# First expert's weights loaded early in a fused S5 / mLSTM / MoE block on Trainium2

## The chip, the cores and the metric

One core of a Trainium2 (trn2) chip runs the whole program in one launch. The metric is the device time in microseconds, lower is better. The engines go by their short names: PE multiplies matrices, ACT and DVE work elementwise, POOL (GpSimd) does small work and the indexed transfers, SP (SyncE) only issues transfers. Each has its own instruction stream, they meet through semaphores, and an engine that waits holds back all that stands behind the wait in its stream.

## What is computed

The reference is one decoder block of width 1024 on 1024 tokens, in float32. What matters here is its last part, the mixture of experts:

```python
logits = t @ w_router + b_router            # t: (1024, 1024), 32 experts
top_vals, top_idx = lax.top_k(logits, 4)
gate = softmax(top_vals)
# for every expert e, over the tokens that chose it:
h = xb @ w_up[e] + b_up[e]                  # (tokens, 2048)
g = minimum(h[:, :1024], 7); lin = clip(h[:, 1024:], -7, 7)
act = g * sigmoid(1.702 * g) * (lin + 1)
y = act @ w_down[e] + b_down[e]             # (tokens, 1024), added to its tokens times gate
```

Ahead of it stand a norm, an input projection, two sequence mixers (mLSTM and S5), the output projection and the router; behind it a last norm.

## The kernel before

`hybrid_block` (L2928) runs five stages one after the other: `project`, `mlstm`, `s5`, `project_out_route` and `experts`. Each is a block of its own with a barrier of all engines at its end, and has its own tiles and semaphores; what must outlive a stage is in `keep_tiles` (L93) or, up to the router, in `mixer_tiles` (L111).

**The route stage**, `project_out_route` (L1523), multiplies the mixers' output by `w_out`, whose 16 pieces come through a ring of four (`raw`, L1531); the last low part of one is made by DVE at L1909 (semaphore `w_lo_done`). Then for each of eight token tiles it norms (result in the first half of `mix["sig_o"]`, called `normed`, stored to DRAM as `t` by SP at L1667), transposes (second half of `sig_o`, called `tT`), makes the logits (PE, L1816 and L1817, semaphore `logits_ready`), takes the top four, and POOL scatters token numbers into a table in DRAM (L1718). SP then stores the residual `h3` tile by tile (L1670), after the fourth of them loads the finished table into SBUF (L1673), and waits for that at the end.

**The expert stage**, `experts` (L2069), goes over the experts in order, in passes of one or two blocks of up to 128 tokens. A pass takes an expert's 12 MB of weights in `CHUNKS` = 12 chunks of 1 MB, 0 to 7 from `w_up` and 8 to 11 from `w_down`. Each chunk takes three steps: SP loads it into a ring of `RAW` = 6 tiles (`load`, L2281), ACT copies its high part into `w_hi` (`hi`, L2493, and `hi_ahead`, L2500; rings of `SPLIT` = 4), DVE makes the low part `w_lo` (`lo`, L2633), and PE multiplies with both (`multiply`, L2825, matmuls at L2868, L2869 and L2872, the bias row at L2878). A load waits for the low part of the chunk six before. The first expert's first six loads wait for nothing:

```python
def load(n, e, j):
    sp.wait_ge(lo_done, n * CHUNKS + (j + 1))
    sp.dma_start(raw[:, j % RAW, :, :], piece(e, j)).then_inc(raw_full[j % RAW], 16)
```

The stage starts with a prologue. POOL gathers the first expert's token rows (L2350) and then loads `b_up` twice into `bias_rows`, 32 rows in partitions 0 to 31 and again in 32 to 63 (L2449). PE turns the token rows (`first_x_turn`, L2897). ACT casts chunk 0 (L2498), makes the high part of the token rows (L2602), casts chunk 1, waits for the bias rows plus one, and copies them (L2607). DVE first waits for the bias rows (L2752) and adds one to a half (L2753), then makes chunk 0's low part (L2635), the token rows' low part (L2759), chunk 1's low part, and the bias rows' low part (L2764). PE's first matmul (L2868) waits for chunk 0's low part and for the token rows' low part. Inside the pass DVE's list, written out by hand in `item` (L2726), has chunk 10's low part at j = 6 ahead of the clamp and product of the hidden half (`hide`, L2685, ops at L2693 and L2700) at j = 7; PE turns that half at L2816 behind chunk 8.

`passes` (L2222) reads the plan of an expert into registers and branches to the pass bodies that it needs, on every engine.

## Time and profile before

| | |
|---|---|
| median of 3 runs | 2300.9 us (2299.7 to 2306.86) |
| the profiled execution's own time | 2290.0 us |
| its span, first to last instruction | 2287.9 us |
| mean granted PE clock | 0.974 of 2.4 GHz |
| PE busy | 2153.6 us, 94% of the span |
| DVE busy | 1616.2 us, 71% |
| ACT busy | 1212.0 us, 53% |
| POOL busy | 549.0 us, 24% |
| DMA | 541.61 MB, 237 GB/s mean |
| expert stage | from 599.2 us to the end |

Times inside the profile are microseconds from the span's start, "mean ns" apart. A row of the timeline has the start, the time (of a merged group), the engine, the line, the operation, output and inputs, and in brackets how long the engine was idle before and what ended it. "SPq" is SP's issuing. The profiled execution took 10.9 us less than the median of the runs, so what is summed from its rows is a difference, to be taken off either.

### The profile page before, as it was taken

Reading aid. Unit: us, or ns where it says so; the run is one execution under the profiler, and the core shown is the slowest. Engines: PE = TensorE matmul, PEld = TensorE weight load, DVE = VectorE, ACT = ScalarE, POOL = GpSimd, SP = SyncE. Lnnn points to the kernel's source line nnn. Section 1 sums busy time; section 2 is a strip of 40 time slices with the busy share of each in tenths; the row PEclk is TensorE's granted clock in tenths of the full one; section 3 lists DMA queues with packets and bytes.
Section 4 is the critical chain, followed back from the end, with each engine's and each line's share of the span. In section 5 each row is a group of like instructions: output and inputs, shape, how many; then the busy total and the mean of one; then the engine's idle time right before and its main releaser. Section 6 shows DMA issues by size and latency. Waiting matters only on the chain.

```text
span 2287.9 us, 32495 instructions
## 1 busy us (share of the span) xinstructions
PE 2153.6 (94%) x10442; PEld 1785.9 (78%) x10443; DVE 1616.2 (71%) x1858; ACT 1212.0 (53%) x1246; POOL 549.0 (24%) x521
## 2 busy tenths in 40 slices
PE   6999986799499999999999999999999999999996
PEld 6787975488378888888888888888888888888874
DVE  4688857546675665779579775877875687677766
ACT  4422243332354554667467564766755576565655
POOL 1001021204411110413134140512511243121304
PEclk9999988999599999999999999999999999999998
DMA  6123263431696675969689895988996699778877
GB/s 181 56 83 135 84 135 129 137 134 65 239 346 190 219 238 200 317 221 379 236 292 373 276 310 202 325 304 280 364 319 215 221 367 336 222 251 293 299 234 263
DMA packets 287300, 541.61 MB, mean 237 GB/s; under 512 B 37302, under 2 KB 53798, under 8 KB 286146
## 3 DMA queue, kind: packets, MB, share of 16 engines
q1 hardware_dynamic: 262770, 494.54, 62.2%
q0 software_dynamic: 24464, 46.24, 8.0%
q8 instruction: 35, 0.57, 0.1%
q14 instruction: 31, 0.25, 0.0%
HBM read 513.61 MB, written 65.13 MB: 253 GB/s over the span
## 4 chain that ended last, share of the span: by engine, by line
PE 56%; issue 6%; DVE 5%; DMA 3%; ACT 3%; ACTq 0%; DVEq 0%; SPq 0%; POOL 0%; POOLq 0%
PE ex_ps_l L2869 8%; PE ex_ps_l L2868 8%; PE ex_ps_g L2869 7%; PE ex_ps_g L2868 7%; PE ex_ps_y L2868 5%; PE ex_ps_y L2869 5%; PE ex_ps_l L2872 4%; PE ex_ps_g L2872 4%; PE ex_ps_y L2872 3%; DVE ex_w_lo L2635 3%; PE ex_ps_t L2806 2%; ACT ex_w_hi L2503 2%; PE ex_ps_t L2816 2%; PE ex_ps_l L2823 1%; DMA ex_raw<-in_w_down_dram 1%
## 5 line engine op out<-in xcount | busy, mean ns | idle before, releaser
L2635 DVE TENSOR_TENSOR ex_w_lo<-ex_raw,ex_w_hi 128x2048 fp32r<-128x2048 f32 x408 | 926.7, 2289 | 371.1 <-ACT ex_w_hi L2503 303.6
L2503 ACT CAST ex_w_hi<-ex_raw 128x2048 fp32r<-128x2048 f32 x371 | 706.4, 1910 | 275.6 <-PE ex_ps_g L2869 99.5
L2342 POOL TENSOR_TENSOR ex_passed<-keep_ident 128x1 f32<-128x1 f32 x136 | 133.6, 982 | 1171.9 <-ACT ex_y L2546 1133.4
L2868 PE MATMUL ex_ps_g<-ex_w_hi,ex_x_hi 128*128 128x512 f32 x784 | 307.3, 392 | 13.0 <-DVE ex_x_lo L2759 11.1
L2868 PE MATMUL ex_ps_l<-ex_w_hi,ex_x_hi 128*128 128x512 f32 x784 | 308.6, 394 | 2.6 <-DVE ex_w_lo L2635 2.6
L2869 PE MATMUL ex_ps_g<-ex_w_lo,ex_x_hi 128*128 128x512 f32 x784 | 305.7, 390 | 0.0
L2869 PE MATMUL ex_ps_l<-ex_w_lo,ex_x_hi 128*128 128x512 f32 x784 | 305.5, 390 | 0.0
L2868 PE MATMUL ex_ps_y<-ex_w_hi,ex_h_hi 128*128 128x512 f32 x544 | 217.5, 400 | 1.7 <-DVE ex_h_lo L2671 1.0
L2869 PE MATMUL ex_ps_y<-ex_w_lo,ex_h_hi 128*128 128x512 f32 x544 | 212.3, 390 | 0.0
L2872 PE MATMUL ex_ps_g<-ex_w_hi,ex_x_lo 128*128 128x512 f32 x544 | 212.2, 390 | 0.0
L2872 PE MATMUL ex_ps_l<-ex_w_hi,ex_x_lo 128*128 128x512 f32 x544 | 212.1, 390 | 0.0
L2868 PEld LDWEIGHTS ex_ps_g<-ex_w_hi,ex_x_hi 128*128 128x128 f32 x784 | 147.6, 188 | 44.0 <-DVE ex_x_lo L2759 11.5
L2868 PEld LDWEIGHTS ex_ps_l<-ex_w_hi,ex_x_hi 128*128 128x128 f32 x784 | 147.2, 188 | 34.6 <-DVE ex_w_lo L2635 5.1
L2869 PEld LDWEIGHTS ex_ps_g<-ex_w_lo,ex_x_hi 128*128 128x128 f32 x784 | 147.6, 188 | 30.1
L2869 PEld LDWEIGHTS ex_ps_l<-ex_w_lo,ex_x_hi 128*128 128x128 f32 x784 | 147.3, 188 | 29.5
L2872 PE MATMUL ex_ps_y<-ex_w_hi,ex_h_lo 128*128 128x512 f32 x424 | 166.0, 391 | 0.0
L2868 PEld LDWEIGHTS ex_ps_y<-ex_w_hi,ex_h_hi 128*128 128x128 f32 x544 | 102.2, 188 | 24.5 <-DVE ex_h_lo L2671 4.9
L2872 PEld LDWEIGHTS ex_ps_g<-ex_w_hi,ex_x_lo 128*128 128x128 f32 x544 | 102.5, 188 | 21.4
L2872 PEld LDWEIGHTS ex_ps_l<-ex_w_hi,ex_x_lo 128*128 128x128 f32 x544 | 102.1, 188 | 21.4
L2869 PEld LDWEIGHTS ex_ps_y<-ex_w_lo,ex_h_hi 128*128 128x128 f32 x544 | 102.3, 188 | 19.7
L2350 POOL DMA_INDIRECT keep_x_rows<-t,ex_gather_at x68 | 110.7, 1628 | 22.3 <-issue 20.6
L601 PE MATMUL pr_acc<-pr_h_hi,pr_w_hi 128*128 128x512 f32 (+1 forms) x240 | 94.8, 395 | 3.9 <-DVE pr_h_lo L655 1.6
(483 smaller groups left out, 3699.0 us busy)
## 6 DMA issues: line engine op xcount, KB each, us to landing
ex_raw<-in_w_up_dram SPq DMA_DIRECT2D x272, 1024.0 KB, 9.2
ex_raw<-in_w_down_dram SPq DMA_DIRECT2D x136, 1024.0 KB, 8.3
st_tab<-tabs SPq DMA_DIRECT2D x8, 1408.0 KB, 7.4
pr_raw<-in_w_in_dram SPq DMA_DIRECT2D x10, 1024.0 KB, 5.5
tabs<-keep_x_rows POOLq DMA_DIRECT2D x16, 256.0 KB, 2.3
tabs<-keep_x_rows SPq DMA_DIRECT2D x16, 256.0 KB, 2.0
por_raw<-in_w_out_dram SPq DMA_DIRECT2D x16, 256.0 KB, 5.3
t<-mix_sig_o SPq DMA_DIRECT2D x8, 512.0 KB, 2.6
```

What stands on the lines that cost most here:

```text
L601: pe.matmul(to, w_hi[:, s, k, cols], h_hi[:, k, toks], start=(k == 0), stop=False)
L2342: pool.tensor_tensor(passed[:, :], ident[:, 0:1], ident[:, 0:1], ALU.add).then_inc(passed_done, 1)
L2350: pool.indirect_dma_start(out=x_rows[:, b, :], out_offset=None, in_=t_dram, in_offset=bass.IndirectOffsetOnAxis(ap=gather_at[:, b:b + 1], ...
L2503: nc.scalar.copy(w_hi[:, j % SPLIT, :, :], raw[:, j % RAW, :, :]).then_inc(hi_done, 1)
L2635: v.tensor_tensor(w_lo[:, j % SPLIT, :, :], raw[:, j % RAW, :, :], w_hi[:, j % SPLIT, :, :].bitcast(F32), ALU.subtract).then_inc(lo_done, 1)
L2806: mm = pe.transpose(to[:, k * P:(k + 1) * P], x_rows[:, b, (4 * half + k) * P:(4 * half + k + 1) * P], ident[:, :])
L2816: mm = pe.transpose(to[:, k * P:(k + 1) * P], hidden[:, row(half, b, blocks), k * P:(k + 1) * P], ident[:, :])
L2823: pe.matmul(to[:, :], lo_in[:, b, 4 * part + k, :], w_hi[:, s, k, :], start=False, stop=False)
L2868: pe.matmul(to[:, :], hi_in[:, b, kk, :], w_hi[:, s, k, :], start=first, stop=False)
L2869: mm = pe.matmul(to[:, :], hi_in[:, b, kk, :], w_lo[:, s, k, :], start=False, stop=last and b > 0)
L2872: mm = pe.matmul(to[:, :], lo_in[:, b, kk, :], w_hi[:, s, k, :], start=False, stop=last)
```

## The change

`EARLY` = 3 chunks of the first expert get their tiles in `keep`, and are loaded in the route stage. `sig_o` moves from `mixer_tiles` to `keep_tiles`, and a new tile `weights` of 1 MB is added there. The other stages, which had tiles of that size of their own, use it too (the second slot of `project`'s weight ring stays its own, the first one is `weights`; `normed` of `mlstm`; `w` of `s5`; the `w_out` ring of the route stage). SP in the route stage loads chunk 0 into `weights` once the last low part of `w_out` is made, chunk 1 into the second half of `sig_o` once all logits are made, and chunk 2 into its first half once the stores of `t` have landed; both of these stand behind the first store of `h3`. In the expert stage SP loads the bias rows ahead of its loop, and for pass number 0 leaves out chunks 0 to 2, by a branch on the pass number that every pass of the loop evaluates. ACT and DVE have the prologue in another order.

```diff
+EARLY = 3
...
 def keep_tiles(nc, ctx):
...
+        "sig_o": sb("sig_o", [P, HEADS, T], F32),
+        "weights": sb("weights", [P, 4, 512], F32),
+        "raw_full": [sem(f"raw_full{i}") for i in range(EARLY)],
...
+def early_tile(keep, j):
+    if j == 0:
+        return keep["weights"][:, :, :]
+    return keep["sig_o"][:, 4 - 2 * j:6 - 2 * j, :].rearrange("p a (b n) -> p (a b) n", n=512)
...
 # project_out_route
-        raw = sb("raw", [P, RING, HALF], F32)
+        raw = keep["weights"]
...
+                sp.wait_ge(w_lo_done, 2 * KD)
+                sp.dma_start(early_tile(keep, 0), weights(p, 0, 0)).then_inc(keep["raw_full"][0], 16)
                 for j in range(TT):
                     sp.wait_ge(scaled, j + 1)
                     sp.dma_start(t_t[:, j, :], normed[:, j % 2, :]).then_inc(normed_out[j % 2], 16)
                 for j in range(TT):
                     sp.wait_ge(acc_read, TT + 2 * j + 2)
                     sp.dma_start(h3_t[:, j, :], h2(j)).then_inc(h3_out, 16)
+                    if j == 0:
+                        sp.wait_ge(logits_ready, TT)
+                        sp.dma_start(early_tile(keep, 1), weights(p, 0, 1)).then_inc(keep["raw_full"][1], 16)
+                        for b in range(2):
+                            sp.wait_ge(normed_out[b], 16 * TT // 2)
+                        sp.dma_start(early_tile(keep, 2), weights(p, 0, 2)).then_inc(keep["raw_full"][2], 16)
                     if j == PLACES_AT:
...
-                for b in range(2):
-                    sp.wait_ge(normed_out[b], 16 * TT // 2)
                 sp.wait_ge(places_in, 16)
...
 # experts: weights(p, e, j) is the old piece(e, j), raw(j) the tile of chunk j
-        raw = sb("raw", [P, RAW, 4, 512], F32)
+        late = sb("late", [P, RAW - EARLY, 4, 512], F32)
...
                 def one_pass(n, e, blocks, plan, kind=None, small=False):
-                    for j in range(CHUNKS):
+                    if e is LAST_E:
+                        for j in range(EARLY):
+                            load(n, e, j)
+                    else:
+                        n = sp.snap(n)
+                        with sp.If(n > 0):
+                            for j in range(EARLY):
+                                load(n, e, j)
+                    for j in range(EARLY, CHUNKS):
                         load(n, e, j)
...
+                for i in range(2):
+                    sp.dma_start(bias_rows[i * E:(i + 1) * E, :], p["b_up"][0]).then_inc(bias_in, 16)
                 with sp.Fori(0, E - 1) as e:
...
                 gather(0, 0, 1)
-                for i in range(2):
-                    pool.dma_start(bias_rows[i * E:(i + 1) * E, :], p["b_up"][0]).then_inc(bias_in, 16)
...
                 hi(0, 0, False)
+                hi(0, 1, False)
+                act.wait_ge(h3_out, 16 * TT)
+                act.wait_ge(bias_plus, 1)
+                nc.scalar.copy(bias_hl[0:2 * E, :], bias_rows[0:2 * E, :]).then_inc(bias_hi_set, 1)
                 for half in range(2):
                     act.wait_ge(t_full, half + 1)
                     nc.scalar.copy(x_hi[:, 0, 4 * half:4 * half + 4, :],
                                    ps_t[half][:, :].rearrange("p (k t) -> p k t", k=4)).then_inc(t_hi, 1)
-                hi(0, 1, False)
-                act.wait_ge(h3_out, 16 * TT)
-                act.wait_ge(bias_plus, 1)
-                nc.scalar.copy(bias_hl[0:2 * E, :], bias_rows[0:2 * E, :]).then_inc(bias_hi_set, 1)
                 hi(0, 2, False)
...
                 choose(0, 0)
+                lo(0, 0)
                 v.wait_ge(bias_in, 32)
                 v.tensor_scalar(bias_rows[0:2 * E, F:2 * F], bias_rows[0:2 * E, F:2 * F], 1.0, None, ALU.add).then_inc(bias_plus, 1)
-                v.wait_ge(bias_plus, 1)
-                lo(0, 0)
+                lo(0, 1)
                 for half in range(2):
...
-                lo(0, 1)
                 v.wait_ge(h3_out, 16 * TT)
+                v.wait_ge(bias_plus, 1)
                 v.wait_ge(bias_hi_set, 1)
```

## Rows read from the trace of the kernel before

**Rows 1.** The chain that ended last, in the expert stage's start (start us, us, what).
```profile
599.40 0.69 SPq L2224
...
600.59 0.47 issue
...
629.76 13.12 DMA ex_raw<-in_w_down_dram
```

**Rows 2.** Busy time by stretch: us, then each engine's, granted PE clock, DMA share, GB/s.
```profile
620.00:640.00 20.00, 20.00 (x88) 16.43 (x87) 18.47 (x11) 13.69 (x10) 0.00 (x0) 0.96 1.04 386
```

**Rows 3.** Timeline of the expert stage's prologue.
```profile
600.65 0.17 ACT L2598 COPY ex_warm<-keep_row_pick 128x1 f32<-128x1 f32 x1
...
602.89 1.10 POOL L2449 DMA_DIRECT2D ex_bias_rows<-in_b_up_dram  x2
...
605.08 1.96 PE L2901 MATMUL ex_ps_t<-keep_ident,keep_x_rows 128*128 128x128 f32 x8 [8.34 <-DMA keep_x_rows<-t,ex_gather_at]
...
607.78 1.90 ACT L2498 CAST ex_w_hi<-ex_raw 128x2048 fp32r<-128x2048 f32 x1 [6.95 <-DMA ex_raw<-in_w_up_dram]
...
609.59 1.06 ACT L2602 CAST ex_x_hi<-ex_ps_t 128x512 fp32r<-128x512 f32 x2
...
613.83 0.73 DVE L2753 TENSOR_SCALAR ex_bias_rows<-ex_bias_rows 64x1024 f32<-64x1024 f32 x1 [14.29 <-DMA ex_bias_rows<-in_b_up_dram]
...
616.41 1.89 ACT L2607 CAST ex_bias_hl<-ex_bias_rows 64x2048 fp32r<-64x2048 f32 x1
616.81 1.28 DVE L2759 TENSOR_TENSOR ex_x_lo<-ex_ps_t,ex_x_hi 128x512 fp32r<-128x512 f32 x2
...
618.14 0.79 PE L2868 MATMUL ex_ps_g<-ex_w_hi,ex_x_hi 128*128 128x512 f32 x1 [11.10 <-DVE ex_x_lo L2759]
```

**Rows 4.** Timeline, end of the first pass.
```profile
642.97 1.90 ACT L2503 CAST ex_w_hi<-ex_raw 128x2048 fp32r<-128x2048 f32 x1 [1.31 <-DMA ex_raw<-in_w_down_dram]
...
647.11 0.68 DVE L2693 TENSOR_SCALAR ex_lin<-ex_ps_l 128x512 f32<-128x512 f32 x1
...
648.65 0.66 PE L2816 MATMUL ex_ps_t<-keep_ident,ex_lin 128*128 128x128 f32 x4 [1.45 <-DVE ex_lin L2700]
```

**Rows 5.** Waits: in the first pass, then 665 to 2250 us (us in total, times, longest).
```profile
PE ex_ps_y L2868 <- DVE ex_h_lo L2671: 1.0, 1, 1.0
...
PE ex_ps_t L2816 <- DVE ex_lin L2700: 6.3, 17, 0.6
...
ACT ex_w_hi L2503 <- DMA ex_raw<-in_w_down_dram: 5.7, 4, 1.8
```

**Rows 6.** Timeline of the route stage, where the early loads are put.
```profile
499.46 0.69 DVE L1909 TENSOR_TENSOR por_w_lo<-por_raw,por_w_hi 128x512 fp32r<-128x512 f32 x1 [2.96 <-ACT por_w_hi L1761]
...
576.61 0.40 PE L1817 MATMUL por_bank<-por_b_router,por_ones_row 1*128 1x32 f32 x2
...
577.77 10.62 SPq L1670 DMA_DIRECT2D h<-mix_v  x2
```

**Rows 7.** DMA issues: count, KB each, median us from issue to landing.
```profile
por_b_down<-in_b_down_dram SPq DMA_DIRECT2D x3, 128.0 KB, 6.1
...
h<-mix_v SPq DMA_DIRECT2D x3, 512.0 KB, 2.6
```

**Rows 8.** Busy time by stretch, columns as in Rows 2, during the bias rows' load.
```profile
608.00:610.00 2.00, 0.00 (x0) 0.00 (x0) 0.00 (x0) 2.00 (x2) 1.11 (x2) 0.50 1.03 229
610.00:612.00 2.00, 0.00 (x0) 0.00 (x0) 0.00 (x0) 0.65 (x2) 0.83 (x4) 0.50 1.03 171
```

**Rows 9.** The clock after a stream of matmuls starts: two stretches, columns as in Rows 2.
```profile
456.00:458.00 2.00, 2.00 (x7) 1.57 (x6) 2.00 (x4) 0.90 (x1) 0.00 (x0) 0.55 1.03 392
...
621.00:622.00 1.00, 1.00 (x5) 0.79 (x4) 1.00 (x1) 0.00 (x0) 0.00 (x0) 0.68 1.05 389
```

**Rows 10.** Timeline, the route stage's first matmul.
```profile
452.33 0.79 PE L1790 MATMUL por_bank<-por_w_hi,por_m_hi 128*128 128x512 f32 x1 [7.17 <-DVE por_w_lo L1909]
```

**Rows 11.** The page's costliest groups: busy, mean ns | idle before, releaser.
```profile
L2635 DVE TENSOR_TENSOR ex_w_lo<-ex_raw,ex_w_hi 128x2048 fp32r<-128x2048 f32 x408 | 926.7, 2289 | 371.1 <-ACT ex_w_hi L2503 303.6
```

More of the change, by code:

```diff
@@ L118, in mixer_tiles @@
         "v": sb("v", [P, NC, HEADS, HD + 1], F32),
-        "sig_o": sb("sig_o", [P, HEADS, T], F32),
+        "sig_o": keep["sig_o"],
         "m_rows": sb("m_rows", [HEADS * NC, CH], F32),
@@ L150, in project @@
         h_lo = sb("h_lo", [P, KD, T], F32R)
-        raw = sb("raw", [P, PRAW, KD, PC], F32)
+        late_pieces = sb("late_pieces", [P, KD, PC], F32)
+        raw = [keep["weights"][:, :, :].rearrange("p a (k n) -> p (a k) n", n=PC), late_pieces]
         w_hi = sb("w_hi", [P, 2, KD, PC], F32R)
@@ L235, in project @@
         loc_set = sem("loc_set")
-        late_raw = raw[:, 1, :, :].rearrange("p k n -> p (k n)")
+        late_raw = late_pieces[:, :, :].rearrange("p k n -> p (k n)")
         gate_rows = late_raw[0:HC, 0:2 * CH].rearrange("k (g t) -> k g t", g=2)
@@ L289, in load_piece @@
                     src = w_in[:, :, at:at + 2 * HEADS].rearrange("p k (g h) -> p k g h", g=2)
[L290 to L291 removed]
+                    sp.dma_start(raw[slot][:, :, 0:HEADS], src[:, :, 0, :]).then_inc(raw_full[slot], 16)
+                    sp.dma_start(raw[slot][:, :, 32:32 + HEADS], src[:, :, 1, :]).then_inc(f_gates_in, 16)
                 else:
[L293 removed]
+                    sp.dma_start(raw[slot][:, :, :], w_in[:, :, at:at + PC]).then_inc(raw_full[slot], 16)
             @block.sync
@@ L410, in hi @@
                         act.wait_ge(piece_used, n - 1)
-                    nc.scalar.copy(w_hi[:, n % 2, :, 0:cols], raw[:, n % PRAW, :, 0:cols]).then_inc(hi_done, 1)
+                    nc.scalar.copy(w_hi[:, n % 2, :, 0:cols], raw[n % PRAW][:, :, 0:cols]).then_inc(hi_done, 1)
                 def square(j):
@@ L979, in mlstm @@
         C = sb("C", [P, 2, HEADS, HD + 1], F32)
-        normed = sb("normed", [P, 2, HEADS, HD], F32)
+        normed = keep["weights"][:, 0:2, :].rearrange("p b (h d) -> p b h d", d=HD)
         denom = sb("denom", [P, NC, HEADS], F32)
@@ L1279, in _, with s5 @@
                 gated(NC - 1)
-def s5(nc, p, g_dram, tabs, mix, st):
+def s5(nc, p, g_dram, tabs, mix, st, keep):
     with ExitStack() as ctx:
@@ L1297, in s5 @@
         g = sb("g", [P, KG, T], F32)
-        w = sb("w", [P, KG, S5W], F32)
+        w = keep["weights"][:, :, :]
         b = sb("b", [P, KG], F32)
@@ L2065, in _, with weights @@
                 plan_with_bias()
+def weights(p, e, j):
+    w_up, w_down = p["w_up"][0], p["w_down"][0]
+    if j < 8:
+        w, half, rows = w_up, (j // 2) % 2 * F + (j // 4) * 512, (j % 2) * 4
+    else:
+        w, half, rows = w_down, (j % 2) * 512, (j // 2 - 4) * 4
+    src = w[bass.ds(e, 1), rows * P:(rows + 4) * P, half:half + 512]
+    return src.rearrange("a (k p) n -> p (a k) n", p=P)
 def experts(nc, p, t_dram, h3_dram, keep, out):
@@ L2107, in experts, with raw @@
         ps_t = [ps(f"ps_t{b}", [P, 512], F32) for b in range(2)]
-        raw_full = [sem(f"raw_full{s}") for s in range(RAW)]
+        raw_full = keep["raw_full"] + [sem(f"raw_full{s}") for s in range(EARLY, RAW)]
+        def raw(j):
+            s = j % RAW
+            return early_tile(keep, s) if s < EARLY else late[:, s - EARLY, :, :]
         hi_done = sem("hi_done")
@@ L2165, in final_tile @@
                 return bias_rows[:, D:2 * D]
-            return raw[:, j // 2 - 2, j % 2 * 2:j % 2 * 2 + 2, :].rearrange("p a n -> p (a n)")
-        w_up, w_down = p["w_up"][0], p["w_down"][0]
-        def piece(e, j):
-            if j < 8:
-                w, half, rows = w_up, (j // 2) % 2 * F + (j // 4) * 512, (j % 2) * 4
-            else:
-                w, half, rows = w_down, (j % 2) * 512, (j // 2 - 4) * 4
-            src = w[bass.ds(e, 1), rows * P:(rows + 4) * P, half:half + 512]
-            return src.rearrange("a (k p) n -> p (a k) n", p=P)
+            return raw(j // 2 - 2)[:, j % 2 * 2:j % 2 * 2 + 2, :].rearrange("p a n -> p (a n)")
         MAIN = E
@@ L2282, in load @@
                     sp.wait_ge(lo_done, n * CHUNKS + (j + 1))
-                    sp.dma_start(raw[:, j % RAW, :, :], piece(e, j)).then_inc(raw_full[j % RAW], 16)
+                    sp.dma_start(raw(j), weights(p, e, j)).then_inc(raw_full[j % RAW], 16)
                 def final_load(j):
@@ L2497, in hi @@
                         act.wait_ge(chunk_used, n * CHUNKS + USED)
-                    nc.scalar.copy(w_hi[:, j % SPLIT, :, :], raw[:, j % RAW, :, :]).then_inc(hi_done, 1)
+                    nc.scalar.copy(w_hi[:, j % SPLIT, :, :], raw(j)).then_inc(hi_done, 1)
                 def hi_ahead(n, j):
@@ L2502, in hi_ahead @@
                     act.wait_ge(chunk_used, n * CHUNKS + (USED + j - SPLIT + 1))
-                    nc.scalar.copy(w_hi[:, j % SPLIT, :, :], raw[:, j % RAW, :, :]).then_inc(hi_done, 1)
+                    nc.scalar.copy(w_hi[:, j % SPLIT, :, :], raw(j)).then_inc(hi_done, 1)
                 def x_high(n, kind, blocks, b, i, rows=P):
@@ L2943, in hybrid_block @@
         with ExitStack() as ctx:
-            mix = mixer_tiles(nc, ctx)
+            mix = mixer_tiles(nc, ctx, keep)
             project(nc, p, u, tabs, lags, rhos, gates, mix, keep)
@@ L2948, in hybrid_block @@
                 mlstm(nc, p, u, tabs, lags, rhos, mix, st, keep)
-                s5(nc, p, g, tabs, mix, st)
+                s5(nc, p, g, tabs, mix, st, keep)
             project_out_route(nc, p, h3, t, table, mix, keep)
```

10 lines of the change are left out of this document (4 added, 6 removed).

## The prediction

> **What bounds the kernel now.** The profile's table comes first: PE is busy 94% of the span, so only stretches in which PE stands still or runs at half clock can give time back, and one of them is the start of the expert stage. The timeline of that prologue shows what it waits for [rows 3]. ACT is free at 600.8 and sits until 607.8 for chunk 0. DVE is free at 599.5 and sits 14.29 us for the bias rows, which POOL asked for at 602.89 and which are there at 613.8. Behind them DVE's list gives chunk 0's low part (2.29 us) and the token rows' low part, and PE's first matmul follows at 618.14. PE had turned the token rows at 605.08 and stood still for 11.10 us.
>
> Then the chain that ended last: from the stage's start to 642.97 it runs through SP and the weight transfers, the last piece of 13.12 us being chunk 10, asked for at 629.76 [rows 1]. Meanwhile the DMA engines are full, at 386 GB/s [rows 2], so a chunk of 1.05 MB takes 2.72 us. The last rows to read are the end of the first pass [rows 4]: chunk 10 lands, ACT casts it at 642.97 (1.90), DVE makes its low part (2.29 [rows 11]), only then come the clamp at 647.11 and PE's turn of the hidden rows at 648.65, for which PE sat idle 1.45 us. So two things bound this pass: PE's start, and the weight stream through chunk 10. Beyond it PE waits little: the same turn costs 6.3 us in 17 waits, 0.37 us each, and ACT waits for weights four times, 5.7 us, in 1585 us [rows 5]. What is won at the end of the first pass should reach the end of the program.
>
> **The three early loads** (route stage, SP). Chunk 0 waits for the last low part of `w_out`, done at 500.2; behind it stands the first store of `t`, which waits for a norm that comes after the right half's matmuls, and a load's issue is short. Chunks 1 and 2 stand behind the first store of `h3` at 577.77. By then the last logits matmul is done (576.61 + 0.40) and so are the stores of `t`, so the added waits are over when SP reaches them; the next store of `h3` comes 10.6 us later [rows 6]. 2.1 MB at 386 GB/s take 5.4 us and are through by about 584, ahead of it. Costed at nothing: the cover is SP's idle time there. If it were gone, the second store of `h3` and with it the table's load would be late; bounds 0 and 5.4 us, taken 0. The other stages share a tile now, in blocks with barriers between them, and no load or op of theirs moves: nothing.
>
> **The bias rows** move from POOL's queue, behind the gathers, to the head of SP's. SP's work in this stage begins at 599.4 [rows 1]. Two issues of some 0.4 us, the second at 599.8. How long the landing takes there no row shows. The nearest from below is a store of 512 KB on an idle queue, 2.6 us [rows 7], landing 602.4; from above the bias load itself today, beside six weight loads, 10.9 us from the first issue [rows 3], landing 610.3. The nearest in shape is `b_down`, also 32 rows into 32 partitions and on SP's queue, 6.1 us [rows 7]: I take that, so 605.9. The Trainium skill, "SBUF — State Buffer", section "Door 1: The DMA port swizzle", says that 32 or 64 partitions reach only half the ports and get 189 or 196 GB/s at 1 MiB against 328 for 128. By that rule, as an estimate, 0.52 MB would take 2.7 us and land near 604.6, and the sum below would start PE 0.8 us sooner. No row has such a load alone; the slow stretch during today's load speaks for it [rows 8].
>
> **PE's start**, by the new order. ACT: chunk 0 cast 600.8 to 602.7 and chunk 1 to 604.6 (1.90 each). DVE: chunk 0's low part 602.7 to 605.0, then it waits for the bias rows to 605.9; queued behind this wait are chunk 1's low part, the token rows' and, through ACT, the bias copy. Plus one 0.73, to 606.7. ACT's bias copy 1.89, to 608.6, now stands ahead of the token rows' high part (1.06 for two, to 609.6), which PE's turn (605.08 + 1.96 = 607.0) no longer holds up. DVE makes chunk 1's low part to 609.0 beside it, and the two token low parts end at 610.4 (half of 1.28 behind ACT's last). PE starts at 610.4 instead of 618.14: **7.7 us earlier**. Bounds of the landing: PE at 609.6 (8.5 us) or 614.7 (3.4 us). [rows 3, 11]
>
> Off it comes the clock. PE's stream at 618.14 ran at 0.50, 1.2 GHz, until the stretch 621 to 622, which is at 0.68, a rise at 621.6, 3.5 us after the start. In the route stage the stream began at 452.33 and the rise was at 457.8 (0.55 over 456 to 458), after 5.5 us [rows 9, 10]. The new start may get either; 2 us more at half the clock cost 1.0 us. Taken **-1.0**, bounds 0 and -1.0. On top comes idle time of the first pass: 1.45 us at the turn, which later passes have at 0.37: **+1.1**, and a wait of 1.0 us for the first hidden half's low part, which no later pass shows [rows 5], +0.9; both because ACT and DVE no longer run at the pace of the landings. PE's side: 7.7 - 1.0 + 1.1 + 0.9 = 8.7 us.
>
> **The stream's side.** Three chunks fewer are 3 x 2.72 = 8.2 us. SP reaches its first weight load later: two bias issues (0.8) and the new branch (0.3, between nothing and the 0.47 us of "issue" beside SP's other branches [rows 1]), -1.1. The bias rows go in the window before the weights instead of into them. Today 608 to 612 run at 229 and 171 GB/s instead of 386 [rows 8], which costs 1.9 us; if the bias rows make all of that it is all won, if the gathers and the small loads do, nothing. Taken half, +1.2, as the four stand in the same stretch. Sum 8.2 - 1.1 + 1.2 = 8.3 us, bounds 7.1 and 9.0. Chunk 10 then lands at 634.7, and the turn follows 5.7 us behind.
>
> The smaller of the two counts: **8.3 us**. Everything behind the first pass shifts as a whole. POOL loses two issues (1.1 us), and gives its memsets and the clearing of `y` earlier; neither is waited for. The profiled execution's 2290.0 becomes 2281.7, the median's 2300.9 becomes **2292.6**.
>
> **The rivals.**
> 1. *Bias rows late.* The prologue turns on the new place of the bias wait: ACT's and DVE's token rows now stand behind it. At today's 10.9 us PE starts at 614.7, 3.4 us sooner, and with idle time won back and the clock against it some 4 us are left: 2296.9. For it: they sat there 14.29 us. Against it: the weight loads are behind them in the same queue. 0.12.
> 2. *The route stage gives some back.* The 2.1 MB run beside the scatters of the table. If these, and the table's load, are held up by the full 5.4 us, 2.9 us are left: 2298.0. Against it: the transfers end some 4 us before the next store [rows 6]. 0.06.
> 3. *Absorbed later, or it doesn't do what it says.* If later passes catch up with the weight stream, an earlier start is lost to the next wait for weights: 2300.9. Against it 5.7 us of such waits in all [rows 5]. 0.06.
> 4. *Slower: the branch.* SP evaluates `n > 0` in 34 passes (408 low parts by 12 [rows 11]). At 0.47 us each [rows 1] that is 16 us, if each is on the path: 2300.9 - 8.3 + 16 = 2308.6. It decides from 0.24 us a pass. It takes effect where the stream is late, and only four waits show that; SP waits for low parts before nearly every load. The Trainium skill speaks for it: "Runtime: NRT & Kernel Launch", section "Instruction fetch mechanics", says that a taken branch to code outside the fetched window stalls for a transfer. The trace has such a pause, but off PE's path. 0.06.
>
> **How the numbers follow.** The forecast has 0.70. Its own range is 2290 to 2294.5: gains from 6.4 to 10.9, the bounds of the landing, the stream and the clock, and a microsecond for the medians. A measurement of this kernel can tell about 0.3%, 6.9 us, from no change, a line at 2294.0. Of the forecast's 0.70 some 0.65 lie below it. Rivals 1 to 3 are within it, save a little of the first: 0.67 faster, 0.27 the same, 0.06 slower. The range 2289.5 to 2299 takes in rivals 1 and 2 and leaves out 3 and 4 and the forecast's tail.
>
> **What would show it.** Right: in the timeline of the new profile ACT's first cast near 600.8 with no wait, the bias rows' plus one near 606, PE's first matmul near 610.4, chunk 10's cast near 634.7, the hidden turn near 640.3, and the expert stage still beginning at 599.2. Wrong: a wait of DVE for bias rows of over 3 us; a stage that begins later; the hidden turn less than 7 us earlier though PE began 8 us earlier (the stream bounds it alone); or a gain at 650 that is not there at the end, with new waits of ACT for weights in later passes.

## The result

Against the kernel before in the same session, ten runs each, the changed kernel takes 2286.96 us (median, 2284.12 to 2293.4) where the one before takes 2300.82. The ratio is 0.9946, interval 0.9935 to 0.9958: **12.4 us faster, 9.7 to 15.0**. The forecast had 2292.6 and a range from 2289.5. The sign and the place of the gain came as forecast, the time lies 2.5 us below the range, and the 8.3 us forecast lie below the interval.

All times below that are written "S + ..." count from the start of the expert stage, where ACT loads its table (599.25 in the profile shown of before, 604.30 in the one of after). The page of after, its first group, hardly moved (the changed kernel's span is 2282.4 us, its profiled execution took 2284.12):

```profile
PE 2153.3 (94%) x10442; PEld 1785.8 (78%) x10443; DVE 1617.7 (71%) x1858; ACT 1210.3 (53%) x1246; POOL 553.7 (24%) x519
```

The prologue does look different. These rows of after's timeline answer to [rows 3]:

```profile
605.78 1.89 ACT L2529 CAST ex_w_hi<-keep_weights 128x2048 fp32r<-128x2048 f32 x1
607.58 1.89 ACT L2529 CAST ex_w_hi<-keep_sig_o 128x2048 fp32r<-128x2048 f32 x1
607.71 2.29 DVE L2666 TENSOR_TENSOR ex_w_lo<-keep_weights,ex_w_hi 128x2048 fp32r<-128x2048 f32 x1 [3.11 <-ACT ex_w_hi L2529]
...
609.84 1.81 POOL L2485 MEMSET ex_y<- 128x2048 f32 x1
609.92 2.27 DVE L2785 TENSOR_SCALAR ex_bias_rows<-ex_bias_rows 64x1024 f32<-64x1024 f32 x1
611.16 1.96 PE L2932 MATMUL ex_ps_t<-keep_ident,keep_x_rows 128*128 128x128 f32 x8 [9.30 <-DMA keep_x_rows<-t,ex_gather_at]
...
612.28 1.90 ACT L2634 CAST ex_bias_hl<-ex_bias_rows 64x2048 fp32r<-64x2048 f32 x1 [2.81 <-DVE ex_bias_rows L2785]
...
614.09 1.05 ACT L2637 CAST ex_x_hi<-ex_ps_t 128x512 fp32r<-128x512 f32 x2
614.70 1.29 DVE L2790 TENSOR_TENSOR ex_x_lo<-ex_ps_t,ex_x_hi 128x512 fp32r<-128x512 f32 x2 [0.31 <-ACT ex_x_hi L2637]
...
616.04 0.79 PE L2899 MATMUL ex_ps_g<-ex_w_hi,ex_x_hi 128*128 128x512 f32 x1 [2.92 <-DVE ex_x_lo L2790]
```

ACT waits for no weights in the prologue any more. The 14.29 us of DVE for the bias rows are gone, and PE starts at S + 11.7, against S + 18.9 in [rows 3]. New is the plus one on the bias rows: 2.27 us where it took 0.73, beside POOL's clearing of `y`. The end of the first pass, which answers to [rows 4]:

```profile
638.72 1.92 ACT L2534 CAST ex_w_hi<-ex_late 128x2048 fp32r<-128x2048 f32 x1 [0.83 <-DMA ex_late<-in_w_down_dram]
...
644.42 0.66 PE L2847 MATMUL ex_ps_t<-keep_ident,ex_lin 128*128 128x128 f32 x4 [0.73 <-DVE ex_lin L2731]
```

That is S + 34.4 for chunk 10's cast and S + 40.1 for PE's turn of the hidden rows, against S + 43.7 and S + 49.4. From 665 to 2250 us the waits are those of [rows 5]:

```profile
PE ex_ps_t L2847 <- DVE ex_lin L2731: 6.2, 17, 0.6
...
ACT ex_w_hi L2534 <- DMA ex_late<-in_w_down_dram: 4.6, 3, 1.7
```

From this turn to the end it takes 1638.0 us, though, where the kernel before took 1639.3. Two things therefore had to be found: what makes the 9.3 us in the first pass, and what is gained behind it with no wait less.

One table for the whole study, read from the timeline of each kernel's profile, in us. "Route" is from ACT's first cast of `m_hi` to S, "first pass" from S to the hidden turn; the ratio is against the kernel before in the same session:

| kernel | route | PE starts | first pass | S to end | ratio |
|---|---|---|---|---|---|
| before | 151.0 | S + 18.9 | 49.4 | 1688.6 | |
| before again | 157.7 | S + 17.0 | 48.6 | 1688.9 | |
| before with 16 increments | 157.8 | S + 17.3 | 48.8 | 1687.2 | |
| before with 48 increments | 157.7 | S + 17.2 | 48.8 | 1687.9 | |
| layout alone | 158.6 | S + 17.6 | 48.8 | 1688.6 | 0.9998 (0.9986 to 1.0011) |
| layout and branch | 157.9 | S + 20.0 | 51.7 | 1691.3 | 0.9999 (0.9990 to 1.0008) |
| bias rows and order alone | 158.6 | S + 20.0 | 48.6 | 1688.2 | 0.9995 (0.9985 to 1.0006) |
| early loads alone | 158.1 | S + 18.2 | 46.6 | 1684.4 | 0.9974 (0.9964 to 0.9984) |
| changed | 158.1 | S + 11.7 | 40.1 | 1678.1 | 0.9946 (0.9935 to 0.9958) |
| changed, again | 157.5 | S + 11.7 | 40.2 | 1678.2 | 0.9949 (0.9931 to 0.9968) |
| changed, 128 increments | 157.0 | S + 11.7 | 40.1 | 1678.4 | 0.9953 (0.9940 to 0.9967) |
| changed, later clearing | 156.3 | S + 10.8 | 40.2 | 1677.6 | |
| changed, token rows first | 157.0 | S + 10.4 | 39.7 | 1677.1 | 0.9951 (0.9936 to 0.9966) |
| changed, old order | 157.8 | S + 10.3 | 39.5 | 1677.3 | 0.9951 (0.9937 to 0.9964) |

### The profile page after: what moved, and what is told of

Read it like the earlier page. It is cut to its first block, busy times and chain, and to the rows that moved or that the text cites. A ratio compares the mean times of both kernels' runs of the same rounds, so it can differ in the third digit from the quotient of the medians.

```text
span 2282.4 us, 32551 instructions
## 1 busy us (share of the span) xinstructions
PE 2153.3 (94%) x10442; PEld 1785.8 (78%) x10443; DVE 1617.7 (71%) x1858; ACT 1210.3 (53%) x1246; POOL 553.7 (24%) x519
## 4 chain that ended last, share of the span: by engine, by line
PE 57%; DVE 6%; issue 6%; ACT 3%; DMA 1%; DVEq 0%; ACTq 0%; POOL 0%; SPq 0%; POOLq 0%
PE ex_ps_l L2900 8%; PE ex_ps_l L2899 8%; PE ex_ps_g L2899 7%; PE ex_ps_g L2900 7%; PE ex_ps_y L2900 5%; PE ex_ps_y L2899 5%; PE ex_ps_l L2903 4%; PE ex_ps_g L2903 4%; PE ex_ps_y L2903 3%; DVE ex_w_lo L2666 3%; PE ex_ps_t L2837 2%; PE ex_ps_t L2847 2%; ACT ex_w_hi L2534 2%; PE ex_ps_l L2854 1%; PE ex_ps_g L2909 1%
## 5 line engine op out<-in xcount | busy, mean ns | idle before, releaser
L2666 DVE TENSOR_TENSOR ex_w_lo<-ex_late,ex_w_hi 128x2048 fp32r<-128x2048 f32 x204 | 463.9, 2288 | 232.2 <-ACT ex_w_hi L2534 164.7
L2534 ACT CAST ex_w_hi<-ex_late 128x2048 fp32r<-128x2048 f32 x170 | 324.5, 1909 | 127.0 <-PE ex_ps_g L2900 60.5
L2666 DVE TENSOR_TENSOR ex_w_lo<-keep_sig_o,ex_w_hi 128x2048 fp32r<-128x2048 f32 x136 | 309.9, 2290 | 109.0 <-ACT ex_w_hi L2534 108.9
L2534 ACT CAST ex_w_hi<-keep_sig_o 128x2048 fp32r<-128x2048 f32 x134 | 255.2, 1904 | 132.5 <-PE ex_ps_g L2900 39.1
L2666 DVE TENSOR_TENSOR ex_w_lo<-keep_weights,ex_w_hi 128x2048 fp32r<-128x2048 f32 x68 | 155.7, 2289 | 33.4 <-ACT ex_w_hi L2534 30.3
L2899 PEld LDWEIGHTS ex_ps_l<-ex_w_hi,ex_x_hi 128*128 128x128 f32 x784 | 147.3, 188 | 34.4 <-DVE ex_w_lo L2666 4.9
L2534 ACT CAST ex_w_hi<-keep_weights 128x2048 fp32r<-128x2048 f32 x67 | 127.6, 1905 | 16.5 <-PE ex_ps_l L2900 12.8
```

Source lines behind the costliest of these rows:

```text
L2534: nc.scalar.copy(w_hi[:, j % SPLIT, :, :], raw(j)).then_inc(hi_done, 1)
L2666: v.tensor_tensor(w_lo[:, j % SPLIT, :, :], raw(j), w_hi[:, j % SPLIT, :, :].bitcast(F32), ALU.subtract).then_inc(lo_done, 1)
L2899: pe.matmul(to[:, :], hi_in[:, b, kk, :], w_hi[:, s, k, :], start=first, stop=False)
```

## Experiments

**The parts of the change.** Four kernels ran in one session, three of them twelve times and the changed one six times. Layout alone keeps the shared tiles and undoes the rest:

```diff
-                sp.dma_start(early_tile(keep, 0), weights(p, 0, 0)).then_inc(keep["raw_full"][0], 16)
...
-                    if e is LAST_E:
...
+                    for j in range(CHUNKS):
                         load(n, e, j)
```

> The changed kernel's tiles (sig_o and weights kept through the program, shared by the stages) with the instruction streams of the kernel before: no early loads, bias rows on POOL, old order of the prologue. Theory A, the gain is all in the first pass of the expert stage: no change, ratio 0.9985 to 1.0015. Theory B, the shared tiles themselves make the stages ahead of the experts faster, which is the 3 us and more of the measured 12 that the first pass of the profile does not show: 3 to 4 us faster, ratio near 0.9985 or below.

Measured: 2299.48 us, ratio 0.9998. The tiles alone do nothing that can be told (3.2 us faster to 2.5 slower).

Early loads alone keeps these and puts the bias rows and both lists of the prologue back:

```diff
-                for i in range(2):
-                    sp.dma_start(bias_rows[i * E:(i + 1) * E, :], p["b_up"][0]).then_inc(bias_in, 16)
                 with sp.Fori(0, E - 1) as e:
...
                 gather(0, 0, 1)
+                for i in range(2):
+                    pool.dma_start(bias_rows[i * E:(i + 1) * E, :], p["b_up"][0]).then_inc(bias_in, 16)
```

> The changed kernel with its bias rows back on POOL's queue and the old order in ACT and DVE; only the early loads stay. If the bias rows set the start of PE alone, they land at about the old time and PE starts at about 14 to 19 us into the expert stage; the shorter weight stream then only saves the idle time in the first pass: 2 to 4 us faster than before, ratio 0.998 to 0.999. If the weight stream is the bound through the first pass, the early loads alone give most of it: 8 us or more, ratio below 0.997.

Bias rows and order alone is the reverse: the bias rows first on SP, the new lists, no early loads (the diff of layout alone as it is printed above, and not the one after it).

> The changed kernel without early loads: bias rows first on SP's queue and the new order in ACT and DVE, all twelve chunks loaded in the expert stage. Chunk 1 lands some 9 us into the stage, the chain through both low parts, the bias copy and the token rows starts PE about 1 us earlier than before. The stream loses 0.8 us at its head and gains up to 1.9 us, since the bias rows no longer run in its middle. 0 to 2 us faster, ratio 0.999 to 1.000. If the bias rows were the main cause, 5 us or more.

And the changed kernel once more:

> The changed kernel again, unchanged, as the measure beside the three others on the same chip: ratio 0.9935 to 0.996, and in its profile the second hidden turn of the first pass 9.3 us earlier after the start of the expert stage than in the kernel before.

Measured: 6.0 us (3.7 to 8.3) for the early loads alone, 1.2 (-1.4 to 3.5) for the bias rows and order alone, 11.7 for both. The parts sum to some 7 us, and by the first passes to 2 of the pair's 8.4. The 6.0 us of the early loads alone are mostly not the first pass: its expert stage is 4.3 us shorter than layout alone's, and about half of that lies at the program's end, which the branch shortens (see below). Neither part does its work in the first pass without the other, and the timelines say why. First the kernel with early loads alone, S = 607.82:

```profile
621.76 0.68 DVE L2784 TENSOR_SCALAR ex_bias_rows<-ex_bias_rows 64x1024 f32<-64x1024 f32 x1 [13.65 <-DMA ex_bias_rows<-in_b_up_dram]
...
626.02 0.80 PE L2899 MATMUL ex_ps_g<-ex_w_hi,ex_x_hi 128*128 128x512 f32 x1 [10.21 <-DVE ex_x_lo L2790]
...
654.45 0.66 PE L2847 MATMUL ex_ps_t<-keep_ident,ex_lin 128*128 128x128 f32 x4 [0.29 <-DVE ex_lin L2731]
```

Then the kernel with the bias rows and order alone, S = 607.74:

```profile
618.45 1.90 ACT L2515 CAST ex_w_hi<-keep_weights 128x2048 fp32r<-128x2048 f32 x1 [9.13 <-DMA keep_weights<-in_w_up_dram]
...
622.17 1.90 ACT L2515 CAST ex_w_hi<-keep_sig_o 128x2048 fp32r<-128x2048 f32 x1 [1.82 <-DMA keep_sig_o<-in_w_up_dram]
...
627.73 0.79 PE L2885 MATMUL ex_ps_g<-ex_w_hi,ex_x_hi 128*128 128x512 f32 x1 [11.43 <-DVE ex_x_lo L2776]
...
656.32 0.66 PE L2833 MATMUL ex_ps_t<-keep_ident,ex_lin 128*128 128x128 f32 x4 [0.30 <-DVE ex_lin L2717]
```

With the early loads the weights are there, but the bias rows land at S + 13.9 and PE starts at S + 18.2. With the bias rows first, these are no longer waited for, but chunk 0, asked for behind them, arrives at S + 10.7 and chunk 1 at S + 14.4. The new order has ACT cast chunk 1 ahead of the bias copy and of the token rows, so here PE's start waits for chunk 1 too, and comes at S + 20.0. In both, PE's idle time at the turn is 0.3 us and 28.4 to 28.6 us pass from PE's start to the turn: PE's start alone bounds the first pass. In the kernels before they are 30.5 and 31.6 us, since there the stream holds PE up. In the old order the start waits for the later of chunk 0 and the bias rows, in the new one for chunk 1 as well. The bias rows first with the old order and without early loads, which would keep chunk 1 out of it, was not run. By an estimate from these rows, chunk 0's low part and the token rows' behind it would start PE near S + 16, but the weight stream would hold the turn: chunk 10's cast stands at S + 43.1 in layout alone, loses 0.8 us to the two issues and wins at most 1.9, so that some 1 us could be gained. That only both together win most of it is shown for the orders that ran.

In the changed kernel the two bounds have met. In its second profile, S = 602.96, chunk 10's cast waits for PE and no longer for the transfer, the turn has 0.29 us of idle time before it instead of 0.73, and the first pass takes the same 40.2 us:

```profile
637.25 1.92 ACT L2534 CAST ex_w_hi<-ex_late 128x2048 fp32r<-128x2048 f32 x1 [0.16 <-PE ex_ps_l L2903]
...
643.16 0.66 PE L2847 MATMUL ex_ps_t<-keep_ident,ex_lin 128*128 128x128 f32 x4 [0.29 <-DVE ex_lin L2731]
```

**Which bound is left.** Three kernels start PE earlier still. The first has one line more, on POOL, against the slow plus one:

```diff
                 pool.wait_ge(bias_zeroed, 1)
+                pool.wait_ge(t_full, 2)
                 pool.memset(y[:, :, :], 0.0).then_inc(y_zeroed, 1)
```

> The changed kernel with one wait more on POOL: it clears y only after the token rows are turned, and so not beside DVE's plus one on the bias rows. Theory that the clearing slows the plus one: it takes 0.7 us instead of 2.3, and with ACT's bias copy and the token rows behind it PE's first matmul comes 1.0 to 1.5 us earlier than S + 11.7 us, while the hidden turn, bound by the weight stream, stays within 0.7 us of S + 40.1. Rival, that the weight loads or the place in the list slow it: 2.3 us still.

Measured (one run; S = 609.12):

```profile
614.74 0.68 DVE L2786 TENSOR_SCALAR ex_bias_rows<-ex_bias_rows 64x1024 f32<-64x1024 f32 x1
...
619.91 0.79 PE L2900 MATMUL ex_ps_g<-ex_w_hi,ex_x_hi 128*128 128x512 f32 x1 [1.40 <-DVE ex_x_lo L2791]
...
649.27 0.66 PE L2848 MATMUL ex_ps_t<-keep_ident,ex_lin 128*128 128x128 f32 x4 [1.30 <-DVE ex_lin L2732]
```

The plus one is back at 0.68 us with the same transfers running: the clearing beside it was the cause. PE starts at S + 10.8, 0.95 us earlier, a touch less than expected, and the hidden turn stays at S + 40.15. What PE won it now waits for at the turn, 1.30 us instead of 0.73.

The second does the same and also takes the token rows' parts ahead of the bias copy (ACT) and of chunk 1's low part (DVE):

```diff
                 hi(0, 1, False)
-                act.wait_ge(h3_out, 16 * TT)
-                act.wait_ge(bias_plus, 1)
-                nc.scalar.copy(bias_hl[0:2 * E, :], bias_rows[0:2 * E, :]).then_inc(bias_hi_set, 1)
                 for half in range(2):
...
+                act.wait_ge(h3_out, 16 * TT)
+                act.wait_ge(bias_plus, 1)
+                nc.scalar.copy(bias_hl[0:2 * E, :], bias_rows[0:2 * E, :]).then_inc(bias_hi_set, 1)
                 hi(0, 2, False)
```

> The changed kernel with ACT making the token rows' high part ahead of the bias rows' copy, DVE the token rows' low part ahead of chunk 1's, and POOL clearing y only after the token rows are turned. Both theories expect PE's first matmul about 2.8 us earlier, near S + 8.9 us instead of S + 11.7 (S: start of the expert stage), and the bias rows' plus one at 0.7 instead of 2.3 us. Theory that the weight stream bounds the first pass now: the hidden turn moves by no more than PE's 0.7 us of idle time before it, S + 39.4 to S + 40.1, the time 0 to 0.7 us below the changed kernel's, which can't be told. Rival, that PE's start bounds it: the hidden turn near S + 37.3 and the time 2.8 us below the changed kernel's.

Measured: 2286.64 us, no different from the changed kernel's; S = 603.35:

```profile
608.97 0.68 DVE L2786 TENSOR_SCALAR ex_bias_rows<-ex_bias_rows 64x1024 f32<-64x1024 f32 x1
...
613.78 0.79 PE L2900 MATMUL ex_ps_g<-ex_w_hi,ex_x_hi 128*128 128x512 f32 x1 [1.40 <-DVE ex_x_lo L2790]
...
643.04 0.66 PE L2848 MATMUL ex_ps_t<-keep_ident,ex_lin 128*128 128x128 f32 x4 [0.55 <-DVE ex_lin L2732]
```

PE starts at S + 10.4, 1.3 us earlier and not the expected 2.8: its turn of the token rows stands at 610.42, S + 7.1, and in the changed kernel the row of that turn names the gather, which no list of ACT and DVE hastens. The gather is itself a side effect that the prediction did not have: in all kernels with the bias rows first that turn stands at S + 6.6 to S + 7.4, in all others at S + 5.7 to S + 6.0. In the changed kernel it costs nothing, since ACT is at the bias copy until later. The hidden turn moves by 0.4 us, inside the 0.7 allowed to it.

The third has the old lists with the bias rows first on SP (the diff is the change's own in ACT's and DVE's prologue, reversed):

> The changed kernel with ACT's and DVE's old order of the prologue (DVE waits for the bias rows first, ACT copies them last), bias rows still first on SP's queue. It shows when the bias rows land, which the changed kernel hides behind chunk 0's low part (at most S + 5.6 us). Theory A, my 6.1 us from the second issue: landing near S + 6.6, plus one, chunk 0's low part to S + 9.8, token rows' low part to S + 11, PE's start S + 11 to S + 12, the time as in the changed kernel within 1 us: then the queue gives the gain and the order nothing. Theory B, that the order matters: PE's start later than S + 13 and the hidden turn and the time over 1 us later than in the changed kernel.

Measured: 2287.52 us; S = 609.03:

```profile
613.67 1.38 DVE L2784 TENSOR_SCALAR ex_bias_rows<-ex_bias_rows 64x1024 f32<-64x1024 f32 x1 [4.34 <-DMA ex_bias_rows<-in_b_up_dram]
...
619.34 0.79 PE L2899 MATMUL ex_ps_g<-ex_w_hi,ex_x_hi 128*128 128x512 f32 x1 [1.40 <-DVE ex_x_lo L2790]
...
648.49 0.66 PE L2847 MATMUL ex_ps_t<-keep_ident,ex_lin 128*128 128x128 f32 x4 [0.60 <-DVE ex_lin L2731]
```

The bias rows land by S + 4.6, 2 us sooner than theory A had it, and the turn comes at S + 39.5. The queue gives the gain; the new order gives nothing. All three bring the turn to between S + 39.5 and S + 40.2, though PE starts 0.95 to 1.4 us earlier, and in all three chunk 10's cast waits for its transfer: with a start ahead of S + 11.7 the stream bounds the pass.

**The branch.** Layout alone, with SP's test of `n > 0` in every pass and the same loads in both arms:

```diff
+                        with sp.If(n > 0):
+                            for j in range(EARLY):
+                                load(n, e, j)
+                        with sp.Else():
+                            for j in range(EARLY):
+                                load(n, e, j)
```

> The layout-only kernel (no early loads, bias rows on POOL, old order) with the branch alone added: on SP every pass but the last tests n > 0 and issues its first three loads in the one arm or, the same three, in the other. Theory that the branch is free and that the code's position sets the pause after SP's last branch (COMPARE_BRANCH to DRAIN, 2.4 us in the kernels without the branch, 0.5 us in those with it): turn of the hidden rows 49 +/- 1 us after the expert stage begins as in the layout-only kernel, the pause at the end 0.5 us, time 0 to 2 us below the kernel before. Rival, that the branch costs and the early loads pay for it too: the hidden turn or the 1639 us behind it grow, by up to 16 us, and the time is over that of the kernel before by 1 us or more.

Measured: 2300.24 us, the time of the kernel before. Its timeline, S = 610.52, and then SP's last branch and its drain behind it (line, op, count, duration in ns, start):

```profile
624.98 1.90 ACT L2526 CAST ex_w_hi<-keep_weights 128x2048 fp32r<-128x2048 f32 x1 [12.88 <-DMA keep_weights<-in_w_up_dram]
...
662.19 0.66 PE L2844 MATMUL ex_ps_t<-keep_ident,ex_lin 128*128 128x128 f32 x4 [2.06 <-DVE ex_lin L2728]
```

```profile
L2279 SPq COMPARE_BRANCH  x1: 50/50/50, 2298.6 to 2298.6; - x1
...
L2292 SPq DRAIN  x1: 62/62/62, 2299.0 to 2299.0; - x1
```

Here both theories missed something. The pause at the end is 0.4 us, as the first had it. But the first pass takes 51.7 us, 2.9 more than with the layout alone, which it had not. SP's second weight load is issued 0.7 us later (S + 4.1 against S + 3.4), which puts it behind POOL's bias rows (S + 3.6) instead of ahead of them, and chunk 0 lands 6 us later, at S + 14.5 against S + 8.4; this is one profile, and why so small a delay costs that much stays open. The changed kernel shows no such thing: SP's first load stands at S + 3.5, 0.86 us later than in the profile of before, of which its two bias loads make 0.81. The later passes show no cost that can be told: from the turn to the issue of the last scatter of `out` it is 1632.2 us, against 1631.7 with the layout alone and 1631.1 and 1632.5 in the two profiles of before. A price of 0.47 us a pass, some 16 us, is excluded, and so are the 0.24 us from which rival 4 would have decided.

**The end of the program.** The expert stage behind the first pass is shorter by 1.3 to 2.4 us in the changed kernel. Up to the issue of the last scatter of `out` nothing can be told apart: the changed kernel's two profiles take 1631.6 us from the turn, between the 1631.1 and 1632.5 of before. The gain lies behind it. From that issue to the end it is 8.1 us in the kernel before (7.9 in its second profile) and 6.4 in the changed one. First before, then after, the same rows of SP:

```profile
L2262 SPq COMPARE_BRANCH  x1: 50/50/50, 2284.0 to 2284.0; - x1
...
L2275 SPq DRAIN  x1: 78/78/78, 2286.4 to 2286.4; - x1
```

```profile
L2285 SPq COMPARE_BRANCH  x1: 50/50/50, 2279.9 to 2279.9; - x1
...
L2298 SPq DRAIN  x1: 53/53/53, 2280.4 to 2280.4; - x1
```

SP jumps over its code for a second wave of rows and arrives 2.4 us later before, 0.5 us later after. All kernels with the new branch have 0.4 to 0.5 us there, layout and branch, which loads nothing early, among them; before, its second profile, layout alone and bias rows alone, which lack it, have 2.3 to 2.6. To ask whether it is the branch itself or only how far it shifts SP's code, lengthen the changed kernel, or lengthen the one before.

```diff
                 sp.wait_ge(h3_out, 16 * TT)
+                for _ in range(128):
+                    sp.sem_inc(pad, 1)
                 last_passes(sp, one_pass)
```

> The changed kernel with 128 short instructions (increments of a semaphore nobody waits for) on SP between its loop and its last passes. They run while SP is far ahead; they only shift where SP's last code lies. Theory that the 1.9 us at the program's end come from the position of SP's jump target: the pause from SP's last COMPARE_BRANCH to its DRAIN changes from 0.5 us, perhaps back to 2.4 us, and the time goes up by that; everything before 2270 us as in the changed kernel. Rival, that the end is shorter because of what the early loads do to the last pass: pause and end stay at 0.5 us and 6.4 us.

Measured: 2288.77 us, pause 2284.9 to 2285.4: 128 leave it short, which says nothing for either. Then the kernel before, with 16 and with 48 such increments, one run each:

> The kernel before with 16 increments of an unused semaphore on SP between its loop and its last passes, and nothing of the change. Theory that the pause from SP's last COMPARE_BRANCH to its DRAIN hangs on where SP's code lies: it moves off the 2.4 us that all kernels without the branch show, here or in the run with 48. Rival, that the branch itself does it: 2.4 us in both.

> The same with 48 increments. Position theory: the pause is not 2.4 us here or in the run with 16, and the end of the program (out's last scatter issue to the last instruction) shortens from 8.1 us by as much as the pause. Rival: 2.4 us and 8.1 us.

Measured, 16 and then 48:

```profile
L2263 SPq COMPARE_BRANCH  x1: 50/50/50, 2296.3 to 2296.3; - x1
...
L2276 SPq DRAIN  x1: 44/44/44, 2296.8 to 2296.8; - x1
```

```profile
L2263 SPq COMPARE_BRANCH  x1: 50/50/50, 2295.5 to 2295.5; - x1
...
L2276 SPq DRAIN  x1: 58/58/58, 2298.0 to 2298.0; - x1
```

With 16 the pause of the kernel before falls to 0.5 us and its end to 6.2; with 48 it is 2.5 and 8.0 again. It is the position, and sixteen useless instructions in the kernel before win at the end what the branch won; with one run each this is read from the profiles' last rows, not from the times. The DMA view of just these stretches shows what goes on in the pause. Before, 2283.9 to 2286.5, with one packet on the instruction queue:

```profile
DMA packets 1, 0.01 MB, mean 3 GB/s; under 512 B 0, under 2 KB 0, under 8 KB 0
...
q14 instruction: 1, 0.01, 1.1%
```

And after, 2279.8 to 2280.5, with none:

```profile
DMA packets 0, 0.00 MB, mean 0 GB/s; under 512 B 0, under 2 KB 0, under 8 KB 0
```

The run with 48 has the packet too and the one with 16 has not. The changed kernel has one a little later, between 2280.5 and 2281.3, behind SP's DRAIN, where no row of SP is late. So a packet comes in both cases, and the position decides whether SP stands still meanwhile; that SP waits for this packet is read from its place and is not shown directly. Layout and branch supports it. Its pause is short, and yet it takes 7.4 us from the last scatter to the end, only 0.7 less than with the layout alone. SP's next rows, in the barrier that ends the stage, are late instead: first layout and branch, then the changed kernel.

```profile
L87 SPq DRAIN  x2: 7/68/130, 2301.1 to 2301.5; - x2
```

```profile
L87 SPq DRAIN  x2: 7/7/7, 2281.2 to 2282.0; - x2
```

The other engines are at this place at 2299.4 and 2281.2. In layout and branch SP comes 1.7 us behind them, and the one packet of the instruction queue lies between 2299.4 and 2301.2: there the pause was not removed but moved.

The Trainium skill, "Runtime: NRT & Kernel Launch", section "Instruction fetch mechanics", says that a taken branch to code outside the fetched window waits for a transfer of it; the rows at SP's last branch agree with that, and put the wait at some 2 us here.

**The profile that the sum was made against.** The kernel before, profiled again:

> The kernel before once more, for a second profile of it. Theory that the profiled execution which the prediction's sum was made against had a short route stage by chance (151.0 us from its first cast of m_hi to the start of the expert stage, against 157.5 to 158.6 in every other kernel's profile, and 10.9 us below its median): this one shows about 158 us there and a span of 2293 to 2297 us, and the expert stage again takes 1688.6 us. Rival, that the early loads make the route stage 7 us longer (they stand in it): 151 us again.

Measured: span 2292.9 us, S = 603.99, expert stage 1688.9, route stage 157.7. Its timeline has a pause of DVE in the route stage that the first profile does not have and after has too (5.61 us at 580.50), and the hidden turn at S + 48.6:

```profile
580.21 1.28 DVE L1983 TENSOR_TENSOR mix_v<-mix_v,por_bank 128x512 f32<-128x512 f32 x2 [5.90 <-remote]
...
652.54 0.66 PE L2816 MATMUL ex_ps_t<-keep_ident,ex_lin 128*128 128x128 f32 x4 [1.44 <-DVE ex_lin L2700]
```

So the early loads do not lengthen the route stage: the first profile was short there by 6.7 us. What the pause waits for, the records do not say.

## Why the prediction was off

**The sum as a whole.** Of the expert stage the profiles give 10.5 us (1688.6 less 1678.1), of which 8.4 to 9.3 lie in the first pass, by which profile of before is taken, and most of the rest, 1.4 to 1.7, at the end. The forecast's 8.3 us for the first pass are therefore nearly right. The step that failed is "everything behind the first pass shifts as a whole": SP's code was shifted too, and the end gained 1.7 us more. With it the forecast would have stood at 2290.9, inside its range, and with all 10.5 us at 2290.4. The measured 2286.96 is 3.4 us below that: 1.9 us are what the ratio's 12.4 has over the 10.5, and 1.5 us come in because the two medians lie 13.9 apart where the ratio says 12.4. So the named step is only part of the miss. The second session says 11.7 us (7.4 to 15.9), and the third, with 128 increments, 10.8 (7.6 to 13.8); 10.5 is inside all three intervals, and whether the remaining 1 to 2 us are real stays open. The profiles can't tell: ACT's first cast of `m_hi` stands anywhere from 445.5 to 453.9 us in the fourteen of them, with kernels before and changed near both ends.

**The three early loads.** Costed at nothing, as they are: route stages of 158.1 and 157.5 us against 157.7. ACT's first cast has no wait.

**The bias rows' landing.** Taken at 6.1 us from the second issue, S + 6.6; it was S + 4.6 at the latest. The nearest row in shape, `b_down`, was a poor guide. The estimate by the Trainium skill's half of the ports ("SBUF — State Buffer", section "Door 1: The DMA port swizzle"), 604.6 on the clock of the profile before, is S + 5.4, nearer to the measured 4.6. Its 2.7 us behind the second issue at 599.8 would make 602.5, though, S + 3.3; for the other 2.1 us the prediction names no source. Any landing before S + 5.6, when DVE is through chunk 0's low part, starts the plus one at the same time; against the S + 6.6 of the forecast that gave 1.0 us back.

**PE's start.** Forecast S + 11.2 (610.4), measured S + 11.7: a gain of 7.2 us, not 7.7. The plus one cost 1.5 us more than its row of before said, of which the early landing took part back; without the clearing beside it the start is S + 10.8. Against the second profile of before, where PE starts at S + 17.0, the gain is 5.2 us and not 7.2: the term hangs on when the bias rows land before, 10.9 us from their issue in the one profile and 9.0 in the other.

**The clock.** Taken at -1.0; it was nothing. PE's stream starts at 616.04, and the stretches (columns as in Rows 2) have the clock at 0.50, 1.2 GHz, until 619, and at 0.91 over the next microsecond, so it rose to 2.4 GHz 3.1 us after the start, where it had taken 3.5:

```profile
618.00:619.00 1.00, 1.00 (x4) 0.81 (x3) 0.97 (x2) 0.74 (x1) 1.00 (x1) 0.50 1.05 396
619.00:620.00 1.00, 1.00 (x5) 0.77 (x5) 1.00 (x1) 0.00 (x0) 0.97 (x2) 0.91 1.07 399
```

**Idle time inside the pass.** Taken at 1.1 + 0.9; from PE's start to the turn it was 30.5 us and is 28.4, a gain of 2.1. PE's side thus came to 7.2 + 2.1 = 9.3, not 8.7; against the second profile of before it is 5.2 + 3.2 = 8.4.

**The stream's side.** Forecast 8.3, bounds 7.1 and 9.0. Chunk 10's cast moved from S + 43.7 to S + 34.4, 9.3 us; against before's second profile, where it stands at S + 42.9, it is 8.5. The first is above the bound of 9.0, the second inside it; the profile that was read had chunk 10 0.8 us later than the other. The refund of 1.9 us for the bias rows' share of the stretch was meant to be taken by half, which is 1.0 and not the 1.2 of the sum; with 1.0 the sum is 8.1. With SP's first load 0.86 us later, 8.2 for the chunks leaves a refund of 2.0 us by the first profile and 1.2 by the second. The branch's 0.3 us were nothing: the two bias issues make 0.81 of the 0.86. That the stream is the smaller side was right in substance, but by a hair: the two sides ended within 0.7 us of each other.

**The rivals.** Bias rows late (1): no, they were there before DVE asked. The route stage giving back (2): no. Absorbed later (3): no, [rows 5] stayed. Slower through the branch (4): excluded by the branch experiment. Its mechanism, a fetch behind a taken branch, is what the end of the program points to, with the other sign: the new code moved an old jump to where nothing is waited for.

**What would show it** asked for a turn near 640.3, 8.4 us earlier; it came 9.3 earlier relative to the stage. That "the expert stage still begins at 599.2" did not hold, and it meant nothing: the kernel before does not begin there either when it is profiled again.

## What to carry to other kernels

When a start waits for two transfers, removing either alone can show next to nothing (2.0 and 0 of 8.4 us in the first pass here); price the pair, and say which side bounds next. Before a sum is made against one profile, compare its time with the median: 10.9 us below it was a warning that a stage of that execution was not typical, and a second profile of the same kernel shows how far the terms themselves vary. And look at the program's end after any edit of an engine's code, since a jump there can gain or lose 2 us that have nothing to do with the work.

## What the runs showed of the hardware

A pause of 2.4 us behind SP's last taken branch comes and goes with the code's length: sixteen short instructions take it away, 48 do not, and the long one has a packet on the instruction queue inside it. Without it the program's end was 1.2 to 1.9 us shorter, less than the pause's 2 us since POOL's drain, done 0.5 us after SP's in the changed kernel, is next; in layout and branch it was 0.7, as SP stood still a little later instead.

DVE's add of a constant on 64x1024 fp32 took 0.68 us alone and 2.27 in the changed kernel, where it started 0.08 us into POOL's clearing of `y`. It ended 0.54 us behind the clearing (609.92 + 2.27 against 609.84 + 1.81), so it waited for that to end rather than run slower beside it. The kernel with the old order shows both sides of this:

```profile
612.71 1.80 POOL L2483 MEMSET ex_bias_hl<- 64x2048 f32 x1
...
614.57 2.24 POOL L2485 MEMSET ex_y<- 128x2048 f32 x1
```

Its add started at 613.67, inside the first clearing, and ended at 615.05, again 0.54 us behind it; and the second clearing, started at 614.57 before the add was through, took 2.24 us instead of 1.81. DVE's low parts, with two inputs, stayed at 2.29 us beside a clearing. The Trainium skill, "SBUF — State Buffer", section "Who interferes with whom", has this as an exclusive lock: whichever of a two-port DVE operation and a GpSimd operation issues first holds the shared ports for the whole instruction. These rows agree.

The bias rows, two loads of 256 KB into 32 partitions each, landed within 4.7 us of the first issue at the head of SP's queue, and took 9.0 to 10.9 us from POOL's, beside SP's weight loads. The store of 512 KB that was taken as the bound from below had 2.6.
